# A hybrid decoder trunk on one NeuronCore: statistics by tile and a norm applied on eviction, between output projection and feed-forward

## The reference

```python
def rmsnorm(x, g):
    return x * lax.rsqrt(jnp.mean(x * x, axis=-1, keepdims=True) + EPS) * g

def swiglu(x, w_gate, w_up, w_down):
    return (jax.nn.silu(x @ w_gate) * (x @ w_up)) @ w_down

y = (b_gate * conv) @ w_out          # layer 0; layer 1: y = o @ w_o
h = h + rmsnorm(y, norm_g[i, 1])     # the post norm
h = h + rmsnorm(swiglu(rmsnorm(h, norm_g[i, 2]), w_gate[i], w_up[i], w_down[i]), norm_g[i, 3])
h = h + jax.nn.sigmoid(h @ w_ple_gate[i]) * (p[i] @ w_ple[i])
```

## Time and profile before

| | us |
|---|---|
| median of 3 runs | 3407.55 |
| the profiled execution | 3402.53 |
| its span | 3400.9 |
| PE busy (matmul) | 3169.6, 93% |
| VectorE busy | 1548.4, 46% |
| ScalarE busy | 824.8, 24% |
| GpSimd busy | 224.9, 7% |
| mean granted PE clock | 0.972 |

### The profile page before, as it was taken

The page is one execution under the profiler, slowest core; times in us unless marked ns, Lnnn a source line. Parts: engine busy times, 40 slices in busy tenths (PEclk is TensorE's granted clock), DMA queues, the critical chain, the costliest instruction groups (busy, mean ns, idle before and its releaser), DMA issues.

```text
span 3400.9 us, 52050 instructions
## 1 busy us (share of the span) xinstructions
PE 3169.6 (93%) x20484; PEld 2996.8 (88%) x20484; DVE 1548.4 (46%) x2500; ACT 824.8 (24%) x1417; POOL 224.9 (7%) x299
## 2 busy tenths in 40 slices
PE   7999969999999997999988998989799999999887
PEld 6999959999999996999987775559699999999887
DVE  5444373433344356433334555443733334433652
ACT  3110231111111122322234553331311111111221
POOL 1000000000000000000034441110000000000000
PEclk9999989999999998999999999999899999999988
DMA  2111101111111111113237657851011111111201
GB/s 86 43 43 49 45 13 50 44 43 44 44 44 45 48 59 31 32 44 115 66 95 159 111 92 268 326 200 44 19 44 45 44 44 45 47 46 44 63 25 59
DMA packets 232954, 238.99 MB, mean 70 GB/s; under 512 B 18661, under 2 KB 190693, under 8 KB 232754
## 3 DMA queue, kind: packets, MB, share of 16 engines
q1 hardware_dynamic: 208770, 155.74, 15.3%
q0 software_dynamic: 23984, 80.30, 8.1%
HBM read 201.11 MB, written 18.10 MB: 64 GB/s over the span
## 4 chain that ended last, share of the span: by engine, by line
PE 87%; DVE 7%; ACT 2%; issue 2%; DMA 1%; POOL 0%; DVEq 0%; ACTq 0%; POOLq 0%
PE psum L1567 20%; PE psum L1569 20%; PE psum L1568 20%; PE psum L1593 5%; PE psum L1587 5%; PE psum L1588 5%; PE psum L1897 2%; PE psum L1942 2%; PE psum L1881 2%; PE psum L1866 1%; DVE psum L1050 1%; DVE y L1056 1%; DVE h L1066 1%; PE psum L1961 1%; PE psum L1991 1%
## 5 line engine op out<-in xcount | busy, mean ns | idle before, releaser
L1567 PE MATMUL psum<-xs_hi,w_hi 128*128 128x384 f32 (+1 forms) x2736 | 893.3, 326 | 8.4 <-DVE w_lo L1025 3.1
L1569 PE MATMUL psum<-xs_hi,w_lo 128*128 128x384 f32 (+1 forms) x2736 | 892.3, 326 | 0.0
L1568 PE MATMUL psum<-xs_lo,w_hi 128*128 128x384 f32 (+1 forms) x2736 | 891.6, 326 | 0.0
L1567 PEld LDWEIGHTS psum<-xs_hi,w_hi 128*128 128x128 f32 x2736 | 513.6, 188 | 10.8 <-DVE y L1264 7.0
L1568 PEld LDWEIGHTS psum<-xs_lo,w_hi 128*128 128x128 f32 x2736 | 513.6, 188 | 0.0
L1569 PEld LDWEIGHTS psum<-xs_hi,w_lo 128*128 128x128 f32 x2736 | 513.5, 188 | 0.0
L1587 PE MATMUL psum<-xs_hi,w_hi 128*128 128x384 f32 (+1 forms) x1104 | 362.8, 333 | 8.5 <-DVE w_lo L1029 4.2
L1588 PE MATMUL psum<-xs_hi,w_lo 128*128 128x384 f32 (+1 forms) x1104 | 359.7, 330 | 0.0
L1569 PE MATMUL psum<-hid_hi,w_lo 128*128 128x384 f32 (+1 forms) x1056 | 346.0, 328 | 0.0
L1568 PE MATMUL psum<-hid_lo,w_hi 128*128 128x384 f32 (+1 forms) x1056 | 345.2, 327 | 0.0
L1567 PE MATMUL psum<-hid_hi,w_hi 128*128 128x384 f32 (+1 forms) x1056 | 344.7, 326 | 0.0
(11 more groups left out here) (257 smaller groups left out, 3653.2 us busy)
## 6 DMA issues: line engine op xcount, KB each, us to landing
kpage<-in_cache_k SPq DMA_DIRECT2D x64, 512.0 KB, 7.2
v_page<-in_cache_v POOLq DMA_DIRECT2D x64, 512.0 KB, 5.7
raw<-in_w_gate SPq DMA_DIRECT2D x44, 512.0 KB, 3.7
raw<-in_w_up SPq DMA_DIRECT2D x44, 512.0 KB, 3.7
raw<-in_w_down SPq DMA_DIRECT2D x44, 512.0 KB, 3.6
raw<-in_w_in SPq DMA_DIRECT2D x24, 512.0 KB, 3.7
raw<-in_w_ple_gate SPq DMA_DIRECT2D x16, 512.0 KB, 3.5
out<-rows_out POOLq DMA_DIRECT2D x16, 512.0 KB, 2.9
```

The costliest lines, as they stand in the source:

```text
L1567: M(out, wh, xh, start=first, stop=False)
L1568: M(out, wh, xl, start=False, stop=False)
L1569: return M(out, wl, xh, start=False, stop=last)
```

## The change

Post norm by tile, inside the last projection block. ScalarE takes each projection tile out of PSUM twice (`take`): its square, and its copy scaled by the gain. VectorE adds squares by tile. PE forms each token's sum with fp32 matmuls whose stationary side is the sum of squares and whose moving side is one column of ones, so the sums stand on partitions, one token each (`token_sums`); ScalarE takes the root of three columns (`deviation`), VectorE their reciprocal (`inverse_dev`), and PE spreads it as a row over all partitions in bank 7 (`token_rows`, three fp32 matmuls with 128 moving columns). VectorE multiplies y by that row and adds it to h, in halves of four chunks.

Second norm late. `xs_hi` and `xs_lo` are now made of h times gain without the reciprocal. ScalarE squares h in halves, GpSimd adds the eight chunks up, and the reciprocal row is kept in `rbB` and applied when gate is taken out of PSUM, and once more to the product with its sigmoid (for up). That stands in every gate block of both feed-forwards. The third statistic's root falls between the first Sigmoids.

Moved: the split of "out"'s second slab goes behind the wait for the conv rows' store; the split of feed-forward slab 1 goes to GpSimd; y's memset behind GpSimd's adds. Cut to its core, with 12 columns of indentation taken off; in order: GpSimd (`joint`, its five adds per tile, the memset), ScalarE (`joint`, `deviation`, the conv rows, the gate blocks), VectorE (`joint`, the gate blocks), PE (`token_sums`, `token_rows`, `last_block`, `first_pair` in place of `first_two`, `last_row` behind the first tile of the third block). Layer 1's "o" gets the same `joint`:

```diff
+def joint(b, ffn_slab):
+    pool.wait_ge(hi_ready, ffn_slab + 2)
+    nc.gpsimd.tensor_tensor(w_lo[(ffn_slab + 1) % RAWS][:, :], raw[(ffn_slab + 1) % RAWS][:, :],
+                            w_hi[(ffn_slab + 1) % HLS][:, :].bitcast(F32), ALU.subtract).then_inc(lo_ready, 1)
+    pool.wait_ge(lo_ready, ffn_slab + 2)
+    for t, (t0, n) in enumerate(TILES):
+        done = 15 * b + 5 * t
+        for half in range(2):
+            x = hsq[half]
+            pool.wait_ge(hsq_ready, 6 * b + 2 * t + half + 1)
+            nc.gpsimd.tensor_tensor(x[:, 0:2, 0:n], x[:, 0:2, 0:n], x[:, 2:4, 0:n], ALU.add)\
+                .then_inc(hsq_summed, 1)
+            pool.wait_ge(hsq_summed, done + 2 * half + 1)
+            if half == 0:
+                nc.gpsimd.tensor_tensor(hs[t][:, 0:n], x[:, 0, 0:n], x[:, 1, 0:n], ALU.add)\
...
+            nc.gpsimd.tensor_tensor(x[:, 0, 0:n], x[:, 0, 0:n], x[:, 1, 0:n], ALU.add).then_inc(hsq_summed, 1)
+            pool.wait_ge(hsq_summed, done + 4)
+            nc.gpsimd.tensor_tensor(hs[t][:, 0:n], hs[t][:, 0:n], x[:, 0, 0:n], ALU.add).then_inc(hsq_summed, 1)
...
+    pool.wait_ge(h_dve, 6 * layer + 6)
     pool.memset(y[:, :, :], 0.0).then_inc(y_zero, 1)
...
+def joint(name, y_, squares, post_row, pre_row, ffn_slab):
...
+    def take(m, t):
+        t0, n = TILES[t]
+        act_e.wait_ge(acc_ready, ready(b0 + m, t))
...
+        dst = ssum if m == 0 else squares[m % 2]
+        A(dst[:, t0:t0 + n], acc(b0 + m, t), ACT.Square).then_inc(tile_squared, 1)
+        A(y_[:, m, t0:t0 + n], acc(b0 + m, t), ACT.Copy, scale=vecT[:, m, post_row:post_row + 1])\
+            .then_inc(acc_free, 1)
...
+    def high(t, half):
+        t0, n = TILES[t]
+        act_e.wait_ge(h_dve, 6 * b + 2 * t + half + 1)
+        for c in range(4 * half, 4 * half + 4):
+            ins = A(xs_hi[:, c, t0:t0 + n], h[:, c, t0:t0 + n], ACT.Copy,
+                    scale=vecT[:, c, pre_row:pre_row + 1])
+        ins.then_inc((xs_half, xs_hi_ready)[half], 1)
...
+    for m in range(C):
+        hi(n0 + m + 1)
+        for t in range(NT):
+            if m < C - 1:
+                take(m, t)
+    A(warm[:, b:b + 1], eps_c[:, :], ACT.Sqrt)
+    take(7, 0)
+    deviation(6 * b)
+    take(7, 1)
+    deviation(6 * b + 1)
+    high(0, 0)
+    take(7, 2)
+    hi(ffn_slab + 1)
+    deviation(6 * b + 2)
+    high(0, 1)
+    h_squares(0, 0)
+    h_squares(0, 1)
+    high(1, 0)
+    high(1, 1)
+    h_squares(1, 0)
+    high(2, 0)
+    high(2, 1)
+    h_squares(1, 1)
+    h_squares(2, 0)
+    deviation(6 * b + 3)
+    h_squares(2, 1)
+    keep_row(6 * b + 3)
+    hi(ffn_slab + 2)
+    deviation(6 * b + 4)
+    keep_row(6 * b + 4)
...
+def deviation(q):
...
+    A(tok_dev[:, c:c + NT], psum[:, 6, c:c + NT], ACT.Sqrt, bias=eps_c[:, :], scale=1.0 / D)\
+        .then_inc(tok_std, 1)
...
-hi_run(SLAB0["out"] + 1, 1)
 for j in range(2):
     act_e.wait_ge(conv_tr, j + 1)
     A(conv_rows[:, 512 * j:512 * j + 512], psum[0:2 + 2 * NB, 6 + j, :], ACT.Copy)\
         .then_inc(conv_rows_done, 1)
 act_e.wait_ge(conv_stored, 32)
-for m in range(C):
-    if m:
-        hi_run(SLAB0["out"] + 1 + m, 1)
-    block_squares("n_mix", y_mix, m, acc_free, ACCS + NT * (BLK0["out"] + m + 1))
-hi_run(SLAB0["ffn0"] + 1, 1)
-norm("n_mix", PAIR, XS0["ffn0"])
+joint("out", y_mix, psq, ROW_G + 1, ROW_G + 2, SLAB0["ffn0"])
...
             for t, (t0, nn) in enumerate(TILES):
-                act_e.wait_ge(acc_ready, ready(blk + 2 * j, t, two))
-                act_e.wait_ge(hid_ready, chunk * NT + (j * NT + t + 1))
-                A(act[:, t0:t0 + nn], acc(2 * j, t), ACT.Sigmoid).then_inc(sig_ready, 1)
-            hi(n + 2 * j + 2, None, i, 12)
+                if two and t == 2:
+                    deviation(6 * layer + 5)
+                    keep_row(6 * layer + 5)
+                act_e.wait_ge(acc_free, blk * NT + (ACCS + 2 * j * NT + t + 1))
+                A(sig[par][:, j, t0:t0 + nn], act[:, t0:t0 + nn], ACT.Sigmoid).then_inc(sig_ready, 1)
+            if two:
+                hi(n + 3)
+            else:
+                hi(n + 2 * j + 2, None, i, 12)
...
+    def sum_tile(m, t):
...
+        V.tensor_tensor(ssum[:, t0:t0 + n], ssum[:, t0:t0 + n], squares[m % 2][:, t0:t0 + n], ALU.add)\
...
+    def scaled(t, half):
...
+        rb = psum[:, 7, 0:n].rearrange("p (o n) -> p o n", o=1).broadcast_to([P, 4, n])
+        V.tensor_tensor(y_[:, k, t0:t0 + n], y_[:, k, t0:t0 + n], rb, ALU.mult).then_inc(y_scaled, 1)
...
+    def added(t, half):
...
+        V.tensor_tensor(h[:, k, t0:t0 + n], h[:, k, t0:t0 + n], y_[:, k, t0:t0 + n], ALU.add).then_inc(h_dve, 1)
+    def low(t):
...
+        for c in range(C):
+            ins = V.scalar_tensor_tensor(xs_lo[:, c, t0:t0 + n], h[:, c, t0:t0 + n],
+                                         vecT[:, c, pre_row:pre_row + 1],
+                                         xs_hi[:, c, t0:t0 + n].bitcast(F32), ALU.mult, ALU.subtract)
...
+    lo(n0 + C)
+    sum_tile(7, 0)
+    inverse_dev(6 * b)
+    sum_tile(7, 1)
+    scaled(0, 0)
+    added(0, 0)
+    inverse_dev(6 * b + 1)
+    tile_ready(b0 + 7, 2, True)
+    scaled(0, 1)
+    added(0, 1)
+    sum_tile(7, 2)
+    scaled(1, 0)
+    added(1, 0)
+    scaled(1, 1)
+    added(1, 1)
+    inverse_dev(6 * b + 2)
+    low(0)
+    scaled(2, 0)
+    scaled(2, 1)
+    added(2, 0)
+    added(2, 1)
+    low(1)
+    low(2)
...
             for t, (t0, n) in enumerate(TILES):
-                tile_ready(blk + 2 * j, t, t == NT - 1, two)
+                if two:
+                    if t == 1:
+                        tile_ready(blk, 2, True, True)
+                        lo(slab + 2)
+                    inverse_dev(6 * layer + NT + t)
+                    dve.wait_ge(row_kept, NT * layer + t + 1)
+                tile_ready(blk + 2 * j, t, t == NT - 1 and not two, two)
+                dve.wait_ge(hid_ready, chunk * NT + (j * NT + t + 1))
+                V.tensor_tensor(act[:, t0:t0 + n], acc(2 * j, t), rbB[:, t0:t0 + n], ALU.mult)\
+                    .then_inc(acc_free, 1)
...
+            for t, (t0, n) in enumerate(TILES):
                 dve.wait_ge(sig_ready, chunk * NT + (j * NT + t + 1))
-                V.tensor_tensor(act[:, t0:t0 + n], act[:, t0:t0 + n], acc(2 * j, t), ALU.mult)\
-                    .then_inc(acc_free, 1)
-            lo(slab + 2 * j + 2, None, i, 12)
+                V.tensor_tensor(act[:, t0:t0 + n], act[:, t0:t0 + n], sig[par][:, j, t0:t0 + n], ALU.mult)\
+                    .then_inc(gated, 1)
+            for t, (t0, n) in enumerate(TILES):
+                dve.wait_ge(gated, chunk * (2 * NT) + (j * 2 * NT + t + 1))
+                V.tensor_tensor(act[:, t0:t0 + n], act[:, t0:t0 + n], rbB[:, t0:t0 + n], ALU.mult)\
+                    .then_inc(gated, 1)
...
+def token_sums(q, src):
...
+    for j, off in enumerate(tok_blocks(t)):
+        c = tok_col(q, j)
+        ins = M(psum[:, 6, c:c + 1], src[:, off:off + P], ones[:, 0:1], start=True, stop=True)
...
+def token_rows(q):
...
+    pe.wait_ge(tok_ready, q + 1)
+    if 0 < k <= NT:
+        pe.wait_ge(y_scaled, 6 * b + 2 * k)
+    elif q:
+        pe.wait_ge(row_kept, NT * b + k - NT)
+    for j, off in enumerate(tok_blocks(q % NT)):
+        c = tok_col(q, j)
+        ins = M(psum[:, 7, off:off + P], tok_inv[:, c:c + 1].broadcast_to([P, P]), ident[:, :],
+                start=True, stop=True)
+    ins.then_inc(row_ready, 1)
...
+        pe.wait_ge(acc_free, blk * NT + t + 1)
+        for c in range(C):
+            if t and c == 4:
+                post_sums(b, t - 1)
+            elif t == 1 and c == 7:
+                token_rows(6 * b)
+            wh, wl = weights(n, slice(c * P, (c + 1) * P))
+            ins = three(acc(blk, t), wh, wl, xh[:, c, t0:t0 + nn], xl[:, c, t0:t0 + nn], c == 0, c == C - 1)
+        ins.then_inc(acc_ready, 1)
...
+    for t in range(NT):
+        pe.wait_ge(acc_free, blk * NT + t + 1)
+        pe.wait_ge(xs_half, NT * layer + t + 1)
+        high(0, t, 0)
+        if t == 0:
+            token_rows(q + 1)
+            post_sums(layer, 2)
+        pe.wait_ge(xs_hi_ready, xs0 + t + 1)
+        high(0, t, 1)
+        if t == 0:
+            token_rows(q + 2)
+            slab(n + 1)
+        elif t == 2:
+            token_rows(q + 3)
+            pe.wait_ge(xs_ready, xs0 + t + 1)
+            low(0, t)
+        pe.wait_ge(acc_free, (blk + 1) * NT + t + 1)
+        high(1, t, 0)
+        high(1, t, 1)
+        if t == 2:
+            pre_sums(layer, 1)
+        else:
+            pe.wait_ge(xs_ready, xs0 + t + 1)
+            low(0, t)
+        low(1, t)
+        if t == 1:
+            pre_sums(layer, 0)
+    token_rows(q + 4)
...
+    def last_row(par, t):
+        if t == 0:
+            pre_sums(layer, 2)
+            token_rows(6 * layer + 5)
```

More of the change, by code:

```diff
@@ L1219, in ffn @@
+            joint("out", y_mix, psq, ROW_G + 2, XS0["ffn0"])
             def ffn(layer):
@@ L1237, in gate_up @@
                                 t0, n = TILES[t]
```

(36 more changed lines are left out.)

138 lines of the change are left out of this document (102 added, 36 removed).

## The result

The changed kernel takes 3365.54 us (median of 4 runs, 3364.19 to 3367.53), the kernel before 3405.89 us beside it: ratio 0.9882, 95% interval 0.9865 to 0.9899. It is faster by 1.2%, 40.3 us. The forecast was 3358, range 3345 to 3376.

What follows compares the result with a forecast made beforehand. VectorE was taken to bound the norm between mixer output projection and feed-forward. Two layers at 28.8 us net give -57.6, the moved slab split +8.2, sum -49.4: profiled 3402.5 to 3353.1, plus 5.0 for the median, forecast 3358, range 3345 to 3376.

Steps and rivals of the forecast that it cites:

- The chain on VectorE: Beside the last projection block and first feed-forward pair: VectorE runs without long gaps and sets the pace until 40.7 us.
- low(0) 4.3, to 30.6: VectorE's xs_lo passes for tile 0 take 4.3 us, ending 30.6 us after the last projection block's start.
- main case: Forecast schedule, fourth feed-forward block at 68.4 instead of 99.2 us; chance 0.60, total 3345 to 3367 us.
- rival (A): VectorE passes with two SBUF inputs and GpSimd's adds exclude each other: 5.2 us per layer, 3361 to 3376; chance 0.25.
- my 54.1: Third feed-forward block starts 54.1 us after the last projection block's first matmul, instead of 87.4.
- Half clock and hand-offs: Allowance in the norm chain for PE's clock halving and hand-offs above 0.12 us: nothing to 4 us, 2.0 taken per layer.
- most of it is hidden: Most of a half-clock stretch on PE between 14 and 27 us costs nothing, since VectorE sets 40.7.
- Token sums and rows: PE's new fp32 matmuls in the norm: 0.9 us for a sum and 0.8 for a row.
- The moved slab split: Layer 0, second "out" block: 6.2 us lost waiting, plus 2.0 of lower clock behind it, 8.2 in sum.
- Table loads: ScalarE's Sqrt between Sigmoids makes three table loads instead of one, 1.28 us each; costs nothing.
- The loop: Feed-forward loop, 44 gate blocks: two more VectorE passes per tile, about 0.55 us each, cost nothing.
- rival (D): The extra gate-block passes stop PE; at 2.0 us a pass, 88 us in all, 3446: slower; chance 0.03.

Runs made afterwards that it cites:

- e2: Changed kernel with GpSimd's fifteen adds of squares per layer left out (partial sums filled with ones, second norm's statistic not computed): 3350.09 us, ratio 0.9841.
- e8: Changed kernel with each GpSimd add of squares replaced by a memset of the same or a larger piece, statistic not computed: 3350.36 us, ratio 0.9846.
- e4: Changed kernel with one more wait, so GpSimd begins its adds of squares behind low(0): 3374.64 us, ratio 0.9921.
- e7: Changed kernel with the edits of e1 and e3, plus useless identity products in three PE waits of each first pair: 3344.85 us, ratio 0.9833.
- e1: Changed kernel with layer 0's split of the second projection slab put ahead of the conv rows again: 3358.98 us, ratio 0.9868.
- e5: Changed kernel without the second multiplication by the reciprocal row in gate blocks but the first chunk's (up not normed): 3365.63 us, ratio 0.9884.
- e3: Changed kernel with GpSimd's adds of squares moved to VectorE, and ScalarE's xs_hi of tile 2 ahead of tile 1's squares: 3354.31 us, ratio 0.9851.

## Why the prediction was right, and where it was not

**Sign and range** held, since the main mechanism is what I said: VectorE's pace and not PE's arithmetic bounded the norms, and a chain on VectorE that runs beside matmuls brings the third block from 87 us behind the last block's start to 61 and 62.

**The chain on VectorE.** Forecast: low(0) begins at 26.3. Measured 26.9 (456.77 - 429.87). Up to there the chain is right to 0.6 us, the exclusion's 0.8 on the add to h among it.

**The step that failed** is "low(0) 4.3, to 30.6" and with it the choice of the main case over rival (A). It took 10.3. In e2, without the adds, it is 4.29 and the third block at 52.8 and 54.3, my 54.1; so the schedule of the forecast is the one without the collision. (A) had a chance of 0.25 and a price of 5.2 us per layer; the price is 8.0 and 8.1. I had let the two engines take turns, and so came to 43.4 for low(1), where it is 47.1 (472.64 and a little more than half of 8.02, less 429.87); the half clock behind the longer wait was not in it at all. The row I leaned on, a memset on GpSimd beside VectorE passes, shows nothing against exclusion: e8 shows that a memset is harmless and an add is not. I had written that a memset reads nothing and still let the row hold (A) at a quarter. The Trainium skill, "SBUF — State Buffer" (Who interferes with whom), says just what e2, e8 and e4 show, with which passes and against which. It deserved to be the likeliest case.

**Half clock and hand-offs, 2.0 per layer.** What e7 gives back is 1.4, which is what the clock costs where it falls on row 1. In the changed kernel it fell there in layer 1 (1.48 us in the timeline above, against 0.83 in layer 0) and explains the 1.6 us between the layers. In layer 0 it cost 1.1 at another place, behind the wait for low(0), which exists only with the collision. My "most of it is hidden" holds elsewhere. So without the collision the clock takes nothing or some 1.4, and not 2.0.

**Token sums and rows, 0.9 and 0.8.** They take 0.59 and 0.67 from start to start (436.13 to 436.72, 448.09 to 448.76). The doubled load width that I feared costs nothing that shows. Two sums and two rows stand between low(1) and the third block and take 0.9 less than forecast, most of the 1.3 by which e2 comes out at 52.8 and not 54.1; the others lie where VectorE sets the pace.

**The moved slab split, 8.2.** Measured 7.6 by the timelines: 6.2 up to the second block, as forecast, and 1.3 of half clock where I took 2.0; e1 gives back 6.6 by the medians. Right.

**Table loads, nothing.** Three loads of 1.28 per layer. ScalarE's timeline after:

```profile
491.50 1.28 ACT L912 ACT_TABLE_LOAD   x1
492.80 0.94 ACT L912 ACTIVATE sig<-act 128x384 f32<-128x384 f32 x2
493.76 1.28 ACT L845 ACT_TABLE_LOAD   x1
495.72 0.26 ACT L845 ACTIVATE tok_dev<-psum,eps_c 128x3 f32<-128x3 f32 x1 [0.68 <-PE psum L1913]
```

The Sigmoid starts 1.30 behind the start of its load, and the Sqrt waits for its sum, not for the load. The 2.66 us per switch of the Trainium skill, "ScalarE: Activation LUTs" (What ACT_TABLE_LOAD costs), shows at none of these loads.

**The loop, nothing.** Right by e5 as far as it can tell; rival (D) is out, passes stay at 0.55.

**Sum.** Forecast -57.6 + 8.2 = -49.4. Measured in the profiled executions: 24.4 (99.30 - 74.85) and 22.8 (99.27 - 76.44) won, 47.3 in all, 7.6 lost at "out", 2.9 in the feed-forwards, 1.8 from the kernel's start, where this run was later; -35.0, of a span shorter by 35.4. The 10.3 us missing from the first term are the exclusion's 16.1, less some 6 us by which the rest of the chain ran ahead of my steps and my allowance. Read by the medians the kernel came out 7.5 above the point, where the ranges of the main case and of (A) overlap. That the main case's own range, 3345 to 3367, holds 3365.5 is luck in part: its schedule without the collision is e2, at 3350, and steps and allowances that were too large made up for some 6 of the 16 us of a collision that it had left out.

## What to carry to other kernels

GpSimd is no free helper for VectorE: in these runs a GpSimd add that reads SBUF and a VectorE op with two SBUF inputs ran nearly one after the other, so adds moved off VectorE cost it most of the time that they take on GpSimd (beside low(0) about 8.5 us of adds cost 6.05), where they are longer besides (a 768-element add 1.86 us in e4 beside a VectorE pass with a PSUM operand, 0.96 on VectorE in e3). Place GpSimd's reads beside VectorE ops with a PSUM operand, or keep them on VectorE in a place off the critical path (the second is e3; a schedule built on the first was not run). And when one instruction moves past a wait (the slab split), count what stands behind it; when PE idles just before a short product that another engine waits for, idle work in front kept its clock (e7).

## What was not expected of the hardware

- The exclusion gives no fixed turns. A GpSimd with adds queued gets in between VectorE's instructions: during low(0) five adds went through at 1.2 to 2.0 us each while VectorE's eight passes took 10.34 us. An add that started while VectorE was in the midst of sixteen passes waited for their end: 5.74 us, with 4.05 of them up to 480.66, across about eight boundaries between instructions (5.75 in layer 1). Why the one gets in and the other does not is open.
- The clock fell behind an idle of 2.7 us between the last block and xs_hi in some layers and not in others (row 1 at 0.83 or 1.48 us with the same kernel), and in neither layer of e7, where the idle was filled.
